# The last layer's sliding attention by groups of four heads' tiles, with column-tile values, a ones column and merged copies

## The reference

```python
def swa_sink_mixer(h, w_in, b_in, sinks, w_out, b_out):
    proj = h @ w_in + b_in
    q, k, v = jnp.split(proj, ...)          # 16 query heads, 2 key/value heads, head size 64
    ...
    s = jnp.einsum('bnqkgd,bnskd->bnkgqs', q, kb).astype(jnp.float32) * (SWA_HEAD_DIM ** -0.5)
    ...
    s = jnp.where(valid[None, :, None, None], s, -jnp.inf)     # window of 128 keys
    mx = jnp.maximum(jnp.max(s, axis=-1, keepdims=True), sink)
    e = jnp.exp(s - mx)
    p = e / (jnp.sum(e, axis=-1, keepdims=True) + jnp.exp(sink - mx))
    o = jnp.einsum('bnkgqs,bnskd->bnqkgd', p.astype(vb.dtype), vb)
    return o.reshape(B, T, SWA_Q_HEADS * SWA_HEAD_DIM) @ w_out + b_out
```

## Time and profile before

| | |
|---|---|
| median of 3 runs | 2404.35 us (2402.65 to 2406.46) |
| the profiled execution | 2404.01 us |
| its span, first to last instruction | 2401.9 us |
| PE busy | 2368.1 us, 99% of the span |
| ACT, POOL, DVE busy | 1047.6, 991.5, 901.8 us |
| mean granted TensorE clock | 0.997 |

### The profile page before, as it was taken

One profiled execution on the slowest core, in us unless ns is written; L12 is line 12 of the kernel. 1 busy time (PEld: TensorE's weight loads), 2 busy tenths in 40 slices (PEclk: granted clock), 3 DMA queues, 4 the chain that ended last, 5 costly groups with the idle time before them and its releaser, 6 DMA issues.

```text
span 2401.9 us, 36465 instructions
## 1 busy us (share of the span) xinstructions
PE 2368.1 (99%) x12886; PEld 1962.1 (82%) x12886; DVE 901.8 (38%) x1817; ACT 1047.6 (44%) x1703; POOL 991.5 (41%) x513
## 2 busy tenths in 40 slices
PE   9999999999999999999999999999999999999999
PEld 6888888888778888888888877788888787888887
DVE  7975322211477742222115233311211874311212
ACT  7565444422346744443335433532332584432321
POOL 4821444444451234444443314544444424444442
PEclk9999999999999999999999999999999999999999
DMA  4311222232320012222332212222222202222221
GB/s 160 113 36 37 97 96 96 96 105 105 125 70 11 3 71 96 96 96 96 105 106 73 94 36 88 88 96 96 96 96 87 71 19 70 96 96 96 96 96 70
DMA packets 57878, 202.95 MB, mean 84 GB/s; under 512 B 7072, under 2 KB 7968, under 8 KB 57392
## 3 DMA queue, kind: packets, MB, share of 16 engines
q1 hardware_dynamic: 55440, 197.07, 23.7%
q10 hardware_dynamic: 2336, 4.50, 0.5%
HBM read 199.44 MB, written 2.10 MB: 84 GB/s over the span
## 4 chain that ended last, share of the span: by engine, by line
PE 70%; issue 15%; POOL 8%; DVE 4%; ACT 2%; DMA 0%; POOLq 0%; ACTq 0%; DVEq 0%
PE bank L859 57%; POOL w_lo L671 7%; PE bank L1125 2%; PE bank L1108 2%; PE bank L1099 2%; PE bank L1226 1%; PE bank L1201 1%; PE bank L1615 1%; PE bank L1212 0%; DVE q_swa L2426 0%; DVE sqacc L2350 0%; PE bank L1596 0%; PE bank L1015 0%; POOL score L787 0%; DVE tmp L2386 0%
## 5 line engine op out<-in xcount | busy, mean ns | idle before, releaser
L671 POOL TENSOR_TENSOR w_lo<-w_raw,w_hi 128x1024 fp32r<-128x1024 f32 x368 | 885.8, 2408 | 1212.8 <-ACT w_hi L1698 1202.9
L859 PE MATMUL bank<-h_hi,w_hi 128*128 128x512 f32 x1616 | 637.7, 395 | 6.2 <-DVE tmp L2799 1.6
L859 PE MATMUL bank<-h_hi,w_lo 128*128 128x512 f32 x1616 | 629.2, 389 | 0.0
L859 PE MATMUL bank<-h_lo,w_hi 128*128 128x512 f32 x1616 | 629.1, 389 | 0.0
L1698 ACT ACTIVATE w_hi<-w_raw 128x1024 fp32r<-128x1024 f32 x368 | 386.8, 1051 | 244.0 <-PE bank L859 220.9
L859 PEld LDWEIGHTS bank<-h_hi,w_hi 128*128 128x128 f32 x1616 | 303.4, 188 | 80.9 <-issue 8.3
L859 PEld LDWEIGHTS bank<-h_hi,w_lo 128*128 128x128 f32 x1616 | 303.4, 188 | 63.8
L859 PEld LDWEIGHTS bank<-h_lo,w_hi 128*128 128x128 f32 x1616 | 303.5, 188 | 63.2 <-issue 2.2
L859 PE MATMUL bank<-mact_hi,w_hi 128*128 128x512 f32 x512 | 199.3, 389 | 1.8 <-DVEq L2652 1.8
L859 PE MATMUL bank<-mact_hi,w_lo 128*128 128x512 f32 x512 | 199.2, 389 | 0.0
L859 PE MATMUL bank<-mact_lo,w_hi 128*128 128x512 f32 x512 | 199.2, 389 | 0.0
(11 more groups left out here) (443 smaller groups left out, 3456.6 us busy)
## 6 DMA issues: line engine op xcount, KB each, us to landing
w_raw<-in_weights SPq DMA_DIRECT2D x368, 512.0 KB, 3.2
x<-in_xT SPq DMA_DIRECT2D x4, 256.0 KB, 6.9
x<-in_xT ACTq DMA_DIRECT2D x4, 256.0 KB, 7.0
memx<-in_memT SPq DMA_DIRECT2D x1, 1024.0 KB, 9.7
cmp_w1k<-in_cmp_w ACTq DMA_DIRECT2D x1, 1024.0 KB, 4.8
cmp_w1v<-in_cmp_w ACTq DMA_DIRECT2D x1, 1024.0 KB, 6.4
out<-x SPq DMA_DIRECT2D x4, 256.0 KB, 2.1
out<-x ACTq DMA_DIRECT2D x4, 256.0 KB, 2.3
```

The lines of the kernel that those rows point to most:

```text
L671: nc.gpsimd.tensor_tensor(w_lo[:, t % RING, :], w_raw[:, t % RAW, :], w_hi[:, t % RING, :].bitcast(F32), ALU.subtract).then_inc(lo_ready, 1)
L859: r = nc.tensor.matmul(out, a, b, start=first and n == 0, stop=last and n == 2)
```

## The change

The 64 units become 16 heads, unrolled, without loops and without staging; the scores of a head use four fixed banks, two of which are the projection's banks 0 and 1. Per round TensorE does the first half's transposes of head+1 (three, tiles 0 and 1), the scores of head+2, the second half's transposes of head+1 (four), and then the values of head+1, in column halves and with a ones column in `sv`. The transposed weights leave PSUM in two copies per head: 384 columns by VectorE (`swa_first_move`) and 512 columns by ScalarE (`swa_second_move`). The row sums come from the ones column, so the exponential no longer accumulates; VectorE adds the sink, GpSimd shifts it (`shift_sink`). The first three scores of head 0 stand inside the product of sq7, the two fillers are gone, GpSimd's last weight rest comes before the attention, and the first output turns stand before the last head's values. The diff, cut:

```diff
-            sv = sb("sv", [P, TT, P], where=s)
+            sv = sb("sv", [P, TT, 2, HD + 1], where=s)
             k_swa = [sb(f"k_swa_{part}", [P, 2, SEQ], F32R, s) for part in ("hi", "lo")]
             q_swa = sb("q_swa", [P, 2 * SWA_PAIRS, SEQ], F32R, s)
-            q_stage2 = sb("q_stage2", [P, 2, SEQ], F32R, s)
-            sink_now = sb("sink_now", [P, 2], where=s)
+            prob_swa = sb("prob_swa", [P, 2, SWA_START[TT]], where=s)
...
+        def swa_part(t, head, first, end):
+            start = 10 * P * (head % 2)
+            return t[:, start + SWA_START[first]:start + SWA_START[end]]
+        def swa_scores_bank(qt):
+            return (score_bank[0], score_bank[1], of(f"sq{KT - 2}"), of(f"sq{KT - 1}"))[qt]
+        def of_unit(t, head, qt):
+            n = TT * (head % 2) + qt
+            return t[:, n:n + 1]
+        def of_head(t, head):
+            return t[:, TT * (head % 2):TT * (head % 2) + TT]
...
+            def shift_sink(head):
+                pool.wait_ge(max_ready, UNIT0["swa"] + TT * (head + 1))
+                if head >= 2:
+                    pool.wait_ge(sink_ready, head - 1)
+                nc.gpsimd.tensor_tensor(of_head(sink_shift, head), of_head(nmax, head), sinks[:, head:head + 1].to_broadcast([P, TT]),
+                                        ALU.add).then_inc(sink_shifted, 1)
...
-            rests(start, end - 1)
-            def first_pair_then_all(at):
-                pool.wait_ge(q_split, 26)
-                attention_begin(at)
-                rests(end - 1, end)
-                pool.wait_ge(q_split, 36)
-            attention_stream(pool, SWA_STREAM, first_pair_then_all, pair_of_heads)
+            rests(start, end)
+            for head in range(SWA_HEADS):
+                shift_sink(head)
...
+            def swa_scores(head, qt):
+                if head:
+                    pe.wait_ge(probs_ready, UNIT0["swa"] + TT * (head - 1) + qt + 3)
+                if qt == 0:
+                    pe.wait_ge(q_split, 2 * 12 + head + 1)
+                kts = key_tiles("swa", qt)
+                out = swa_scores_bank(qt)[:, 0:P * len(kts)]
                 for part, k in enumerate(k_swa):
-                    r = nc.tensor.matmul(out[:, 0:n], q, k[:, l, kts[0] * P:(qt + 1) * P], start=part == 0, stop=part == 1)
+                    r = nc.tensor.matmul(out, q_swa[:, head, qt * P:(qt + 1) * P], k[:, head // 8, kts[0] * P:(qt + 1) * P],
+                                         start=part == 0, stop=part == 1)
                 r.then_inc(scores_ready, 1)
 
...
+            def swa_transposes(head, half):
+                pe.wait_ge(probs_ready, UNIT0["swa"] + TT * head + 2 * half + 4)
+                if head:
+                    pe.wait_ge(swa_moved[half], head)
+                for c in range(SWA_START[2 * half], SWA_START[2 * half + 2], P):
+                    to = c - SWA_START[2 * half]
+                    r = nc.tensor.transpose(probT_bank[half][:, to:to + P], prob_swa[:, head % 2, c:c + P], ident[:, :])
+                r.then_inc(swa_turned, 1)
+            def swa_values(head):
+                if head >= 2:
+                    pe.wait_ge(swa_out, head - 1)
+                sums = o_bank[head % 2][:, 0:TT * (HD + 1)].rearrange("p (a n) -> p a n", a=TT)
+                for qt in range(TT):
+                    if qt % 2 == 0:
+                        pe.wait_ge(swa_moved[qt // 2], head + 1)
+                    weights, kts = swa_part(probT_groups, head, qt, qt + 1), key_tiles("swa", qt)
+                    for n, kt in enumerate(kts):
+                        for rows in (slice(0, HD), slice(HD, P)):
+                            r = nc.tensor.matmul(sums[rows, qt, :], weights[:, n * P + rows.start:n * P + rows.stop], sv[:, kt, head // 8, :],
+                                                 start=n == 0, stop=n == len(kts) - 1)
+                r.then_inc(swa_valued, 1)
+            def swa_round(head):
+                if head + 1 < SWA_HEADS:
+                    swa_transposes(head + 1, 0)
+                if head + 2 < SWA_HEADS:
+                    for qt in range(TT):
+                        swa_scores(head + 2, qt)
+                if head + 1 < SWA_HEADS:
+                    swa_transposes(head + 1, 1)
+            def swa_concat():
+                t = CHUNK["mix1.0"]
+                def turn(j):
+                    pe.wait_ge(swa_out, 2 * j + 2)
+                    turn_output(2, "scat", o_tok2, j)
+                turn(0)
+                turn(1)
+                swa_values(SWA_HEADS - 1)
+                turn(2)
+                turn(3)
+                bank_free(JOB["mix1.0"])
+                chunk_ready(t)
+                for k in range(KT):
+                    pe.wait_ge(cat_split, KT * 2 + k + 1)
+                    r = three(of("mix1.0")[:, :], slot(t, k), (h_hi[:, k, :], h_lo[:, k, :]), k == 0, k == KT - 1)
+                    if k + 4 < KT:
+                        turn(k + 4)
+                r.then_inc(chunks_used, 1)
...
-                    for j in range(2, KT):
+                    for j in range(2, KT - 1):
                         column_tile(f"sq{j}")
+                    def first_two_scores():
+                        pe.wait_ge(first_query_moved, 2)
+                        pe.wait_ge(k_split, 13)
+                        for qt in range(2):
+                            swa_scores(0, qt)
+                    def third_scores():
+                        wait_evacuated(pe, f"sq{KT - 2}")
+                        swa_scores(0, 2)
+                    around(f"sq{KT - 1}", {2: first_two_scores, 5: third_scores})
                     wait_evacuated(pe, "svT")
-                    pe.wait_ge(first_query_moved, 2)
-                    pe.wait_ge(k_split, 13)
-                    def banks_free():
-                        for j in (KT - 2, KT - 1):
-                            wait_evacuated(pe, f"sq{j}")
-                    attention_stream(pe, SWA_STREAM, lambda at: attention_begin(at, banks_free), pair_of_heads)
-                    concat(2, "scat", "swa1", UNIT0["swa1"] + 32, "mix1.0", (h_hi, h_lo))
+                    swa_transposes(0, 0)
+                    wait_evacuated(pe, f"sq{KT - 1}")
+                    swa_scores(0, 3)
+                    for qt in range(TT):
+                        swa_scores(1, qt)
+                    swa_transposes(0, 1)
+                    for head in range(SWA_HEADS - 1):
+                        swa_values(head)
+                        swa_round(head)
+                    swa_concat()
...
+            def swa_exponentials(head, qts):
+                for qt in qts:
+                    act.wait_ge(max_ready, UNIT0["swa"] + TT * head + qt + 1)
+                    if head >= 2:
+                        act.wait_ge(swa_turned, 2 * (head - 2) + qt // 2 + 1)
+                    weights = prob_swa[:, head % 2, SWA_START[qt]:SWA_START[qt + 1]]
+                    nc.scalar.activation(weights, swa_scores_bank(qt)[:, 0:P * len(key_tiles("swa", qt))], ACT.Exp, bias=of_unit(nmax, head, qt),
+                                         scale=-1.0).then_inc(probs_ready, 1)
+            def swa_second_move(head):
+                act.wait_ge(swa_turned, 2 * head + 2)
+                if head >= 2:
+                    act.wait_ge(swa_valued, head - 1)
+                weights = swa_part(probT_groups, head, 2, 4)
+                nc.scalar.activation(weights, probT_bank[1][:, 0:SWA_START[4] - SWA_START[2]], ACT.Copy).then_inc(swa_moved[1], 1)
+            def sink_exponential(head):
+                act.wait_ge(sink_shifted, head + 1)
+                if head >= 2:
+                    act.wait_ge(swa_out, head - 1)
+                nc.scalar.activation(of_head(sinkexp, head), of_head(sink_shift, head), ACT.Exp).then_inc(sink_ready, 1)
...
+                    swa_exponentials(0, range(TT))
+                    for head in range(-1, SWA_HEADS - 1):
+                        if head >= 0:
+                            sink_exponential(head)
+                        if head + 2 < SWA_HEADS:
+                            swa_exponentials(head + 2, (0, 1))
+                        swa_second_move(head + 1)
+                        if head + 2 < SWA_HEADS:
+                            swa_exponentials(head + 2, (2, 3))
+                        if head == 0:
+                            act.wait_ge(swa_biased, KT + 2)
+                            round_queries("swa", KT - 1, sq_q[:, KT - 1, :])
+                    sink_exponential(SWA_HEADS - 1)
+                    act.wait_ge(swa_valued, SWA_HEADS)
...
+            def swa_maximum(head, qt):
+                dve.wait_ge(scores_ready, UNIT0["swa"] + TT * head + qt + 1)
+                if head >= 2 and qt == 0:
+                    dve.wait_ge(sink_shifted, head - 1)
+                n = P * len(key_tiles("swa", qt))
```

(57 more changed lines are left out.)

203 lines of the change are left out of this document (10 added, 193 removed).

## The result

The changed kernel takes 2407.95 us (median of 22 runs, 2404.60 to 2410.29) and the kernel before, run beside it, 2404.43 (22 runs, 2400.99 to 2409.88). The ratio is 1.0013 with a 95% interval of 1.0007 to 1.0019: 3.5 us slower. That is clear of the scatter, but less than the 0.2% (4.8 us) that the forecast counted as a difference. The forecast was 2409.0 us, with "within 0.2%" as the likeliest case.

A forecast was written before the change was run, and what follows sets the result against it. A closed loop of handoffs, 3.55 us a head, was to bound the attention, not TensorE's 2.95; the stage 3.2 us longer plus 1.5 for the clock, 4.7 in all, gave a median of 2409.0 us, range 2398.5 to 2413.0.

The forecast's parts named there:

- TensorE's own work: Transposes, scores and values of one head in the last layer's attention: 2.9 to 3.0 us against 3.25 before.
- V: A head's value matmuls, 14 pairs of records: 0.97 us, with TensorE standing 0.4 to 0.7 us inside for ScalarE's second move.
- T1: A head's second-half transposes on TensorE, four of them, between the next head's scores and V: 0.58 us.
- T0: A head's first-half transposes on TensorE, three of them, which open its round: 0.35 to 0.45 us.
- The ring: Closed loop of handoffs through TensorE, VectorE and ScalarE from one T0 to the next: period 3.55 us against 3.25 before.
- B: Rival: TensorE stays the bound and is faster, period 2.95 us, stage 5.2 us shorter, 2399.2 us; chance 0.18.
- C: Rival: longer loop, slower 384-column copy and later second move, period 3.75 us, 2.8 us more, 2411.9 us; chance 0.15.
- The rests after head 0: VectorE does both rests of tile 6's queries after head 0; its slack covers half, so 0.7 us once.
- The beginning: Stage start: VectorE's second rest of tile 5 collides with GpSimd's weight rest; without that lock 2.1 us shorter.
- The clock: Idle wait of some 3.2 us before the first T0 may halve TensorE's clock for heads 0 and 1: 1.5 us more.
- A: Main forecast: loop-bound at 3.55 us with the clock lost once, 4.7 us more, 2409.0 us; chance 0.38.
- A': Same as A without a clock loss: 3.2 us more, 2407.6 us; chance 0.29.

The follow-up runs named there:

- e_lag: Changed kernel with each head's values put behind the next head's transposes and scores, and VectorE's output one head later: 2400.02 us, 0.9980 of before.
- e_lag_full: e_lag without column halves, one value matmul of all 128 columns per key tile and query tile: 2404.86 us, 0.9994 of before.
- e_order2: Changed kernel with ScalarE's second move put before the exponential of the next group's tile 1: 2404.20 us, 0.9991 of before.
- e_split2: Changed kernel with the merged second move split into two copies of 256 columns, each waited for separately: 2406.28 us, 1.0003 of before.
- e_extra2: Changed kernel with two useless 256-column matmuls added inside each values part, before the third query tile: 2408.38 us, 1.0017 of before.
- e_late_rest: Changed kernel with GpSimd's last weight rest held back until VectorE's rests of tile 5 are done: 2406.22 us, 1.0010 of before.
- e_lag_late: e_lag with GpSimd's last weight rest held back until VectorE's rests of tile 5 are done: 2397.83 us, 0.9972 of before.
- e_order_split: Changed kernel with the edits of e_order2 and e_split2 together: 2403.32 us, 0.9986 of before.
- e_full2: Changed kernel without column halves, one value matmul of all 128 columns per key tile and query tile: 2414.37 us, 1.0039 of before.

## Why the prediction was right
- **TensorE's own work** (2.9 to 3.0 us): 2.82, as e_lag shows, where nothing on TensorE waits. V 0.96 for a forecast 0.97, T1 0.53 for 0.58, T0 0.31 for 0.35 to 0.45; the scores 1.02 for 1.03.
- **Where that saving comes from**: this was wrong in part. The forecast named the column halves and the fewer changes of kind, four a head in place of twelve. e_lag_full has the fewer changes without the halves, and its 3.22 are only 0.03 under before's 3.25; the halves give 0.40, although they make the changes that are left dearer by 0.15. The sum did not need the split.
- **The ring** (3.55): 3.53. Every term came within 0.03 us: 0.59 for 0.59, 0.47 for 0.48, 0.27 and 0.40 for 0.28 and 0.41, 0.55 for 0.18 + 0.36, 1.26 for 1.25. The standing in V was put at 0.4 to 0.7 and is 0.5. The chain from the memory heads carried over whole, and e_order2, e_split2, e_extra2 and e_lag each took one link away, shortened it or filled the hole, with the change in period that the ring gives. Rivals B (2.95) and C (3.75) are ruled out as periods.
- **The rests after head 0** (0.7 us once): from T0 of head 1 to that of head 15 are 50.4 us, 14 x 3.53 and 1.0 more; 0.7 of it is in the period from head 2 to head 3, which is 4.26 long.
- **The beginning**: both rests at 2.8 us, as forecast. In after's trace all is 3.0 us earlier; with these 3.0 added, the last matmul of tile 7's product was to end at 1923.9 and does at 1923.7, the first T0 was to come at 1927.1 and does at 1927.3, T0 of head 1 was to come at 1931.7 without a clock loss and comes at 1932.6 with one. e_late_rest could not test the second rest, but e_lag_late did: with that rest free of the collision the first T0 comes 2.0 us sooner, where the forecast had 2.1. The idle piece is 3.59, put at 3.2.
- **The end** (4.4 us from T0 of head 15 to the projection): 4.45.
- **The clock** (+1.5): the mechanism was right, the size not, since the stretch at half clock was 3.4 us and not as long as in the earlier trace rows. It cost 0.8 to 0.9. The stage is 4.2 us longer where 4.7 was forecast with a loss and 3.2 without one.

3.5 us in the medians lie between cases A and A'. The two differ by whether the clock falls, and each kernel with an idle piece of 3.5 us there shows a fall in its one trace, of 3.4 to 10.2 us. The forecast was 1 us too high, most of it that term. No large errors cancel in it: every other term of the sum is within 0.3 us of its measure.

What the forecast didn't see is how cheap the ring was to open: with the values one period later, the same change is 0.20% faster than before, and with the held-back weight rest 0.28%.

## What to carry to other kernels
When work is grouped to spare a busy engine, write down the ring of handoffs from one group's first instruction to the next group's and compare it with the engine's own sum: the longer of the two is the period. If the ring is longer, move an in-order neighbour's step one place up, split the copy that the engine waits for, or let the consumer lag by one group; each is a few lines, and here they gave 0.30, 0.16 and 0.71 us of a period of 3.53. A merged copy saves its own engine an instruction and takes from the waiting one the half that it could have started on.

## What the runs showed of the hardware that I had not expected
- The values of one key tile and one query tile take 0.137 us as two matmuls on 64-column halves (seven such pairs in the 0.96 us of e_lag's V) and 0.216 us as one on all 128 columns (seven in e_lag_full's 1.51). Each matmul is two records. In e_lag's trace the records of the two halves start within 0.01 us of each other and the next two 0.06 later; in e_lag_full's a record starts every 0.11 us. So the halves overlap. The Trainium skill, page "TensorEngine Tiling (Array Packing)", section "Key Properties", says that different tiles can load weights and multiply in parallel; the pair agrees. Passing from transposes to such halves and back costs 0.15 us a head.
- After nearly the same idle time ahead of the first T0 (3.5 to 3.65 us) the granted clock was at 0.50 for 3.4 us (after, e_lag_full), 6.8 us (e_order2, e_extra2, e_split2, e_order_split) or 10.2 us (e_full2). After 2.5 us idle it fell in e_lag and not in e_late_rest; in the three kernels with 1.53 us or less it stayed at 1.00. The same is seen ahead of everything that changed: near 1856 us it was at 0.50 for 6.8 us in two of the thirteen traces, for 3.4 us in eight, and not at all in after, e_order2 and e_lag. One execution each; what decides it stays open.
- The order in which VectorE's and GpSimd's rests meet isn't fixed. With the same code up to there, tile 2's two rests took 1.40 us in after and in most others, and 5.58 in e_lag and e_late_rest; from there on the collisions fell on tiles 3 and 5 in the first case and on tiles 2 and 4 in the second.
